# Fetching a block of tokens as half rows into all 128 partitions

## The reference

```
logits = x @ router_w + router_b;  top_vals, top_idx = top_k(logits, 4);  gates = softmax(top_vals)
h = x_pad[tok] @ w1[e] + b1[e]                       # 1024 -> 2048, for the tokens of expert e
h = min(h[:1024], 7) * sigmoid(1.702 * min(h[:1024], 7)) * (clip(h[1024:], -7, 7) + 1)
out = (h @ w2[e] + b2[e]) * gate                     # 1024 -> 1024, added to the token's row
```

## Time and profile before

| | |
|---|---|
| time, median of 3 runs | 1314.32 us (1312.75 to 1316.9) |
| span of the profiled execution | 1311.8 us |
| TensorE, VectorE, ScalarE, GpSimd busy | 1035.8, 266.2, 190.4, 156.6 us |
| bytes moved by DMA | 445.04 MB, mean 339 GB/s |
| software queue (GpSimd's DMAs) | 8512 packets, 22.32 MB |

### The profile page before, as it was taken

How to read it: one execution, slowest core, us unless ns; L and a number is a source line. 1 busy time by engine, 2 the same in 40 slices (tenths; PEclk the granted TensorE clock), 3 DMA queues, 4 the chain that set the end, 5 groups by cost and what they waited for, 6 DMA issues and landing times.

```text
span 1311.8 us, 13342 instructions
## 1 busy us (share of the span) xinstructions
PE 1035.8 (79%) x4653; PEld 414.8 (32%) x4654; DVE 266.2 (20%) x620; ACT 190.4 (15%) x372; POOL 156.6 (12%) x202
## 2 busy tenths in 40 slices
PE   5965898997778779778877877788777787787793
PEld 4734444332222223222222222222222222222231
DVE  2996525111111101111111101000111111111112
ACT  3543411111111101111111001011111111111111
POOL 0670001010001001000000000000000000000000
PEclk9987888998888889988888888888888888888896
DMA  9702664899999959999999999999999999999993
GB/s 320 272 1 51 218 254 171 307 385 392 394 395 395 393 187 377 394 395 394 393 394 393 393 395 393 394 396 397 392 397 399 397 392 396 395 395 392 355 322 96
DMA packets 123459, 445.04 MB, mean 339 GB/s; under 512 B 6323, under 2 KB 13903, under 8 KB 123420
## 3 DMA queue, kind: packets, MB, share of 16 engines
q1 hardware_dynamic: 114788, 422.15, 83.2%
q0 software_dynamic: 8512, 22.32, 7.0%
q10 hardware_dynamic: 144, 0.38, 0.1%
HBM read 431.33 MB, written 14.84 MB: 340 GB/s over the span
## 4 chain that ended last, share of the span: by engine, by line
DMA 50%; PE 39%; DVE 8%; issue 1%; SPq 1%; ACT 1%; POOLq 0%; DVEq 0%; POOL 0%; ACTq 0%
DMA W<-in_w_dram 48%; PE PS L897 22%; PE PS L877 6%; DVE WA L962 3%; PE PS L769 3%; DVE WA L959 2%; PE PS L644 1%; SPq L295 1%; PE PS L871 1%; PE PS L595 1%; DMA WA<-in_state_conv_dram 1%; PE PS L823 1%; DMA acc_rows<-XT,scol 0%; PE PS L762 0%; PE PS L679 0%
## 5 line engine op out<-in xcount | busy, mean ns | idle before, releaser
L897 PE MATMUL PS<-W,XT 128*64 128x512 f32 x1056 | 292.0, 715 | 161.8 <-DMA W<-in_w_dram 160.5
L877 PE MATMUL PS<-WB,X 128*64 128x512 f32 x1088 | 239.5, 592 | 0.0
L877 PE MATMUL PS<-WA,X 128*64 128x512 f32 x1024 | 226.7, 595 | 0.0
L897 PEld LDWEIGHTS PS<-W,XT 128*64 128x64 f32 x1056 | 96.7, 165 | 335.9 <-issue 335.9
L1158 DVE TENSOR_SCALAR X<-PS 128x512 f32<-128x512 f32 x33 | 22.8, 692 | 695.5 <-PE PS L877 695.5
L1293 POOL DMA_INDIRECT acc_rows<-XT,scol x33 | 52.2, 1582 | 749.6 <-ACT XT L576 749.6
L877 PEld LDWEIGHTS PS<-WB,X 128*64 128x64 f32 x1088 | 82.1, 137 | 151.4 <-issue 151.4
L877 PEld LDWEIGHTS PS<-WA,X 128*64 128x64 f32 x1024 | 77.4, 138 | 144.1 <-issue 144.1
L576 ACT ACTIVATE XT<-PS,wtab 128x512 f32<-128x512 f32 x33 | 22.7, 687 | 446.5 <-PE PS L897 446.5
L871 PE MATMUL PS<-b1q,XT 128*64 128x512 f32 x264 | 70.4, 608 | 1.5 <-DVE XT L1152 1.5
L1165 DVE TENSOR_SCALAR X<-PS 128x256 f32<-128x256 f32 x66 | 24.9, 420 | 212.7 <-PE PS L877 212.7
(11 more groups left out here) (223 smaller groups left out, 567.5 us busy)
## 6 DMA issues: line engine op xcount, KB each, us to landing
WA<-in_w_dram SPq DMA_DIRECT2D x64, 2048.0 KB, 24.5
WB<-in_w_dram SPq DMA_DIRECT2D x64, 2048.0 KB, 24.7
W<-in_w_dram SPq DMA_DIRECT2D x64, 2048.0 KB, 19.3
WB<-in_w_in_dram SPq DMA_DIRECT2D x5, 1024.0 KB, 12.0
WB<-in_w_in_dram SPq DMA_DIRECT2D x1, 2048.0 KB, 14.4
W<-in_w_out_dram SPq DMA_DIRECT2D x1, 2048.0 KB, 18.0
W<-in_w_out_dram SPq DMA_DIRECT2D x2, 1024.0 KB, 9.7
acc_rows<-X POOLq DMA_DIRECT2D x3, 512.0 KB, 7.2
```

The costliest lines, as they stand in the source:

```text
L877: last = mm(PS[64 * n:64 * n + 64, 1 + s, :], xTe[:, SLOTS * k:SLOTS * k + SLOTS], w1buf[u][:, c, k % 4, 512 * n:512 * n + 512], start=Fal ...
L897: last = mm(PS[64 * n:64 * n + 64, 3, :], hT[:, s, h, :], w2buf[:, 4 * h + s, 512 * n:512 * n + 512], start=(s == 0 and h == 0), stop=(s = ...
```

## The change

A block is fetched as half rows of 2048 bytes: the source is h_dram seen as rows of 512, the index is the scatter's column of stab, and the destination is all 128 partitions, so that partition p gets half p // 64 of slot p % 64. The bound of the index is 2 * TOK - 1 = 639 and an index beyond it is passed over, so pads, which point at 640 and up, are not fetched and keep what was there; their gate is zero. Four transposes of 128x128 turn x, and gain_x puts the two halves in place as it reads. gtab and the operation that makes it go; tab_ok counts to 5.

```diff
-        gtab = sb("gtab", [SLOTS, MAXB], U32)
...
-        gcol = sb("gcol", [SLOTS, 1], U32)
+        gcol = sb("gcol", [P, 1], U32)
...
-        xg = Xf[0:SLOTS, 0:1024]
+        xg = Xf[:, 0:512]
...
+        h_halves = h_dram.rearrange("t (h n) -> (t h) n", h=2)
...
-            sp.wait_ge(S["tab_ok"], 6)
+            sp.wait_ge(S["tab_ok"], 5)
...
             def turn_x():
-                for k in range(KD):
-                    last = tp(PS[:, 0, SLOTS * k:SLOTS * k + SLOTS], xg[:, P * k:P * k + P], ident[0:SLOTS, 0:SLOTS])
+                for k in range(KD // 2):
+                    last = tp(PS[:, 0, P * k:P * k + P], xg[:, P * k:P * k + P], ident)
                 last.then_inc(xtp_ready, 1)
...
-            v.tensor_scalar(gtab[:, :], t1[0:SLOTS], -1.0, 0.0, ALU.add, ALU.max).then_inc(S["tab_ok"], 1)
...
             def gain_x():
-                v.tensor_tensor(xTe.rearrange("p (k s) -> p k s", k=KD), PS[:, 0, :].rearrange("p (k s) -> p k s", k=KD),
-                                bc(par[:, 8:16], SLOTS), ALU.mult).then_inc(xT_ready, 1)
+                v.tensor_tensor(xTe.rearrange("p (h k s) -> p h k s", h=2, k=KD // 2),
+                                PS[:, 0, :].rearrange("p (k h s) -> p h k s", h=2, k=KD // 2),
+                                bc(par[:, 8:16].rearrange("p (h k) -> p h k", h=2), SLOTS), ALU.mult).then_inc(xT_ready, 1)
...
-            hmax = pool.to_reg(TPAD - 1)
+            hmax = pool.to_reg(2 * TOK - 1)
...
             def gather(m):
-                g.indirect_dma_start(out=xg, out_offset=None, in_=h_dram[:, :],
+                g.indirect_dma_start(out=xg, out_offset=None, in_=h_halves,
                                      in_offset=bass.IndirectOffsetOnAxis(ap=gcol[:, 0:1], axis=0),
-                                     bounds_check=hmax, oob_is_err=True).then_inc(xg_ready, 16)
+                                     bounds_check=hmax, oob_is_err=False).then_inc(xg_ready, 16)
...
-                g.tensor_copy(gcol[:, :], gtab[:, bass.ds(m + 2, 1)]).then_inc(turn, 1)
+                g.tensor_copy(gcol[:, :], stab[:, bass.ds(m + 2, 1)]).then_inc(turn, 1)
```

More of the change, by code:

```diff
@@ L561, in _ @@
             act.copy(GT[:, :], PS[0:E, 5, 0:TPAD]).then_inc(S["gt_ok"], 1)
-            act.wait_ge(S["tab_ok"], 6)
+            act.wait_ge(S["tab_ok"], 5)
             total = act.value_load(cnt_i[0:1, 2 * E:2 * E + 1], min_val=E, max_val=MAXB - 2)
@@ L849, in _ @@
             keep_clock(6)
-            pe.wait_ge(S["tab_ok"], 6)
+            pe.wait_ge(S["tab_ok"], 5)
             pe.wait_ge(xg_ready, 16)
@@ L1138, in _ @@
             v.tensor_scalar(inv, t1, 0.0, C[:, C_S1:C_S1 + 1], ALU.is_equal, ALU.mult)
-            v.tensor_scalar(gtab[:, :], t1[0:SLOTS], -1.0, 0.0, ALU.add, ALU.max).then_inc(S["tab_ok"], 1)
             own(v.tensor_scalar(t2, t1, 2.0, C[:, C_S2:C_S2 + 1], ALU.mult, ALU.add))
             v.tensor_tensor(stab[:, :], t2, inv, ALU.add).then_inc(S["tab_ok"], 1)
-            dve.wait_ge(S["tab_ok"], 6)
+            dve.wait_ge(S["tab_ok"], 5)
             def gain_x():
-                v.tensor_tensor(xTe.rearrange("p (k s) -> p k s", k=KD), PS[:, 0, :].rearrange("p (k s) -> p k s", k=KD),
-                                bc(par[:, 8:16], SLOTS), ALU.mult).then_inc(xT_ready, 1)
+                v.tensor_tensor(xTe.rearrange("p (h k s) -> p h k s", h=2, k=KD // 2),
+                                PS[:, 0, :].rearrange("p (k h s) -> p h k s", h=2, k=KD // 2),
+                                bc(par[:, 8:16].rearrange("p (h k) -> p h k", h=2), SLOTS), ALU.mult).then_inc(xT_ready, 1)
             dve.wait_ge(xtp_ready, 1)
@@ L1253, in _ @@
                 pool.dma_start(h_dram[P * i:P * i + P, :], Hs(i)).then_inc(h_out[i], 16)
-            pool.wait_ge(S["tab_ok"], 6)
+            pool.wait_ge(S["tab_ok"], 5)
             for i in range(NT):
@@ L1272, in _ @@
                     pool.wait_ge(xtp_ready, 1)
-                g.tensor_copy(gcol[:, :], gtab[:, m:m + 1]).then_inc(turn, 1)
+                g.tensor_copy(gcol[:, :], stab[:, m:m + 1]).then_inc(turn, 1)
                 pool.wait_ge(turn, m + 2)
```

## The result

The changed kernel takes 1283.85 us (1283.4 to 1285.3), the one before 1314.24 us beside it: a ratio of 0.9776, 95% interval 0.976 to 0.9792. The profiled execution has a span of 1283.5 us.

What follows compares the result with a forecast made beforehand. The DMA queue was taken to set the pace from 240 to 1225 us, through the wait for W2. Gathers -18.0, TensorE -1.4, VectorE -0.1, GpSimd +0.5 summed to -19.0 us: 1295 us, range 1286 to 1309.

Steps and rivals of the forecast that it cites:

- The bound and the path: From 240 to 1225 us the DMA engines set the pace; less work in the queue lands W2 earlier.
- The cause of the double cost: The gather costs 1.21 us, its bytes only 0.64; the extra was read as writing to one half of the partitions.
- The saving of 0.58 us a gather: Gather: 0.62 us instead of 1.2, ends 0.49 and 0.77; over 31 gathers 18.0 us.
- The gather of before, 1.2 us: Price from weights not moved beside one gather: 0.50 MB missing at 410 GB/s, 1.21 us.
- The gather after, 0.62 us: Taken between 0.43 us (even spread, pads free) and 0.71 (all 8 pieces on an engine), nearer the upper end.
- The price of a piece, 0.089 us: Cost of 2048 bytes, taken from a load of w_in to all partitions: 187 packets in 1 us.
- The small terms: TensorE's transposes -1.4 us, VectorE's dropped operation -0.1, GpSimd's issue of the first gather +0.5: -1.0 us.
- The sum: -18.0 - 1.4 - 0.1 + 0.5 = -19.0 us, giving 1295 us, 1.4% less.
- Pieces cost more: Rival: pieces dearer than 0.089 us, a gather 0.73 up to 1.05 us; 1299 to 1309 us, chance 0.17.
- no change: Rival: indexed fetching is slow whatever the partitions, pads keep their place; gather stays 1.2 us, 1313 us, chance 0.12.
- slower: Rival: pieces cost 0.166 us like the scatter's, or 0.180; 1317 to 1321 us, chance 0.07.
- more saved: Rival: pads free, even spread counts, 0.77 us saved a gather, 24.9 us in all; 1289 us, no separate chance.

Runs made afterwards that it cites:

- The placements: Changed kernel with its slots placed on the partitions in other orders: reversed 1284.15 us, even 1281.86, packed 1287.21, beside 1283.43 unchanged.
- the first three runs: Kernel before with pads skipped, 1299.23 us; changed kernel with pads fetched, 1293.37; kernel before with its whole rows into partitions 32 to 95, 1296.53.
- The even placement: Changed kernel with slots dealt out in turn over the eight runs of four partitions of a half: 1281.86 us, ratio 0.9769 to the kernel before.

## Why the prediction was wrong

*The bound and the path.* Right. The queue sets the pace before and after (share 1.03), W2 is still waited for, and where bytes or slowness left the queue the end time followed. One reading was off: the 23 to 25 us in the chain are the transfer of W2, while TensorE itself stood waiting for it some 6 us a time (160.5 us in 27 waits from 300 to 1280 us).

*The cause of the double cost.* Right, and shown apart from the pads and from the index: 64 rows moved up by 32 partitions cost their bytes and no more.

*The saving of 0.58 us a gather.* This is the step that failed: both prices in it were mis-sized, the one after more than the one before. The end time has 0.96 us a gather, the stretch that W2 paces 0.79 to 0.89 (25.8 to 22.9 us over 29 gathers).

*The gather of before, 1.2 us.* Too small: 1.36 us in the end time, 1.30 in the stretch. The 1.21 us was worked out with 410 GB/s as the rate of weights without a gather; the stretch just ahead of it has 421, and with that rate the same 1.06 MB give 3.8 - 1.06/0.421 = 1.28 us. 31 * 0.10 to 31 * 0.16, 3 to 5 us of the miss. Whether the rest is slowness that outlasts the 3.8 us is left open.

*The gather after, 0.62 us.* Too large: 0.40 us in the end time, 0.42 to 0.52 in the stretch, so 31 * 0.10 to 31 * 0.22, 3 to 7 us of the miss. The price of a piece, 0.089 us, was near: with pads fetched a packet of two pieces took at most 0.176 * 3.8 * 16 / 64 = 0.167 us, some 0.08 a piece, and at that the even spread of 77.6 pieces is 0.39 us. What was mis-sized is the allowance on top of it for the fullest engine, from 0.43 to 0.62, near to eight pieces, though the fullest holds 6.6 on average (33 blocks counted by expert from the reference's inputs). The placements show that the fullest engine does count, so the direction of the allowance was right; at 0.08 us 6.6 pieces would still be 0.53 us, and why the end shows less stays open. Pads are close to free: skipping them, from 18.4 to 28.5 us saved, gave 0.33 us a gather, where 50.4 pieces at 0.08 us on 16 engines are 0.25.

*The small terms.* -1.0 us was forecast for them; with nothing fetched the two kernels can't be told apart (1270.43 against 1270.8 us). The start was forecast to lose 0.5 us to the first gather and gained: its 3 us, with the granted clock of 1.00 instead of 0.87, are a term that the sum didn't have but for 0.2 us a turn. TensorE's four transposes take 0.65 us, not 0.52; the first gather lands 1.0 us sooner instead of 0.5 later, since with 24 tokens in the block less is fetched (with pads fetched it takes 3.80 us, as before); GpSimd's issue grew by 0.1 us (1241 against 1143 ns), not 0.44.

*The sum.* 19.0 us were forecast, 28.5 and 30.4 measured in two sets of runs. In the first profiles the span is 28.3 us shorter: 22.9 in the stretch that W2 paces, some 3 at the start, 1.6 ahead of the routing tables, where the two kernels do the same work, and 0.9 behind the last W2. Both errors of the price had the same sign, which the range did not allow for: its low end came from the lowest price after (0.43 us, 1289 us, and 3 us of room), with no error on the price before.

*The rivals.* "Pieces cost more", "no change" and "slower" are refuted by the first three runs; "more saved" was nearest, and still too small.

## What to carry to other kernels

Where the DMA queue sets the pace, price a small transfer by what the large stream didn't move beside it, with the rate just ahead of it as well as just behind it, and put an error on that price too. Here 0.26 MB fetched to partitions 0 to 63 slowed the weights beside it and cost 1.3 us; the same bytes at partitions 32 to 95 cost 3.8 - 1.29/0.41 = 0.65 us, their share. When indexed pieces are skipped, try dealing the filled ones out over the engines: at the scatter that gave 5 to 6 us on top of the 8 from skipping.

## What the runs showed that was not expected

Two half rows fetched by index to neighbouring partitions went as one packet of 4096 bytes (8512 packets with 128 pieces a gather as with 64), while the scatter's additions stay at 128 packets a block: the 4112 packets of the software queue between 600 and 1200 us are 19 gathers of 80 and 18 scatters of 144. The Trainium skill's page "DMA: Bandwidth & Descriptors", section "SWDGE vs HWDGE vs iDMA", calls a packet of up to 4096 bytes the preferred one, which the plain fetch agrees with and the adding scatter doesn't.

A pad that is skipped by index isn't absent from the queue: it is a packet under 512 bytes. The 35 gathers have 2240 - 1280 = 960 slots without a token. With whole rows and pads skipped the page has 960 more such packets than before (7283 against 6323), one for each. In the changed kernel it has 944: 16 of the 33 blocks hold an odd number of tokens, and in each of their halves one skipped piece shares its packet with a fetched one, so that one small packet less is made for the block. The even placement, which parts neighbours, has fewer still (7154).
